# Zero products between the steps at the beginning of the experts: 24, 6, 15 and 14 in place of 14, 4 and 8

## The reference, cut to what matters

```python
def moe_swiglu(x, w_router, w_in, w_out):
    xf = x.reshape(B * S, D)
    logits = (xf @ w_router).astype(jnp.float32)
    top_v, top_i = lax.top_k(logits, TOP_K)          # TOP_K = 2
    w = jax.nn.softmax(top_v, axis=-1)
    gate = jnp.sum(jax.nn.one_hot(top_i, N_EXPERTS) * w[..., None], axis=1)
    out = jnp.zeros((B * S, D), jnp.float32)
    for e in range(N_EXPERTS):
        out = out + gate[:, e:e + 1] * swiglu(xf, w_in[e], w_out[e])
    return out.reshape(B, S, D)
```

## Time and profile before

| | us |
|---|---|
| median of 3 runs | 2832.63 (2832.41 to 2834.3) |
| profiled execution, its own time | 2832.4 |
| its span in the trace | 2830.6 |
| mean granted TensorE clock | 0.968 of full |
| PE busy | 2676.8 (95%) |
| DVE busy | 2113.2 (75%) |
| ACT busy | 1615.6 (57%) |

### The profile page before, as it was taken

The page is one execution under the profiler, slowest core; times in us unless marked ns, Lnnn a source line. Parts: engine busy times, 40 slices in busy tenths (PEclk is TensorE's granted clock), DMA queues, the critical chain, the costliest instruction groups (busy, mean ns, idle before and its releaser), DMA issues.

```text
span 2830.6 us, 39691 instructions
## 1 busy us (share of the span) xinstructions
PE 2676.8 (95%) x12900; PEld 2161.0 (76%) x12900; DVE 2113.2 (75%) x2501; ACT 1615.6 (57%) x2109; POOL 21.5 (1%) x39
## 2 busy tenths in 40 slices
PE   7899999988999999999999888999999999999997
PEld 5677778776777787877997666788878878888875
DVE  6765677676666756866546856699989888999998
ACT  3545544455554444444444543577778777777776
POOL 0000000000000000000000000000000000000000
PEclk9999999999999999999999978899999999999999
DMA  8655468665454655644554411899989999999995
GB/s 315 208 163 167 157 225 263 224 194 176 171 164 142 231 180 177 201 145 157 190 181 156 144 38 45 289 360 335 362 310 366 331 349 336 343 355 331 364 353 214
DMA packets 193794, 666.09 MB, mean 235 GB/s; under 512 B 23056, under 2 KB 34960, under 8 KB 193024
## 3 DMA queue, kind: packets, MB, share of 16 engines
q1 hardware_dynamic: 189760, 647.66, 65.6%
q0 software_dynamic: 3904, 16.76, 1.8%
HBM read 663.29 MB, written 1.05 MB: 235 GB/s over the span
## 4 chain that ended last, share of the span: by engine, by line
PE 81%; DVE 9%; ACT 4%; DVEq 2%; issue 2%; DMA 1%; SPq 0%; ACTq 0%
PE ps L467 45%; PE ps L473 22%; DVE wlo L1971 3%; PE ps L487 2%; PE ps L566 2%; ACT whi L1383 1%; PE ps L492 1%; DVE mod_sum L1995 1%; PE ps L1263 1%; DMA ada_raw<-in_w_ada 1%; PE ps L665 1%; PE ps L777 1%; DMA proj<-in_w_ada 1%; PE ps L707 1%; DVEq L2422 0%
## 5 line engine op out<-in xcount | busy, mean ns | idle before, releaser
L1971 DVE TENSOR_TENSOR wlo<-raw,whi 128x1024 fp32r<-128x1024 f32 x709 | 862.2, 1224 | 445.4 <-ACT whi L1383 433.3
L1383 ACT ACTIVATE whi<-raw 128x1024 fp32r<-128x1024 f32 x709 | 746.1, 1059 | 664.4 <-PE ps L473 588.4
L467 PE MATMUL ps<-whi,xh 128*128 128x512 f32 (+3 forms) x1248 | 454.4, 374 | 4.0 <-issue 4.0
L467 PE MATMUL ps<-whi,xl 128*128 128x512 f32 (+3 forms) x1248 | 443.1, 365 | 0.0
L467 PE MATMUL ps<-whi,gathered_hi 128*128 128x512 f32 x896 | 362.6, 405 | 5.3 <-ACT whi L1383 2.8
L467 PE MATMUL ps<-whi,gathered_lo 128*128 128x512 f32 x896 | 356.0, 397 | 0.0
L473 PE MATMUL ps<-wlo,xh 128*128 128x512 f32 (+3 forms) x1248 | 293.9, 362 | 0.0
L473 PE MATMUL ps<-wlo,gathered_hi 128*128 128x512 f32 x896 | 283.3, 397 | 0.1
L467 PEld LDWEIGHTS ps<-whi,xh 128*128 128x128 f32 x1248 | 239.2, 192 | 43.8 <-issue 6.1
L467 PEld LDWEIGHTS ps<-whi,xl 128*128 128x128 f32 x1248 | 239.8, 192 | 36.3 <-issue 1.7
L473 PEld LDWEIGHTS ps<-wlo,xh 128*128 128x128 f32 x1248 | 216.4, 191 | 38.8
(11 more groups left out here) (420 smaller groups left out, 3586.9 us busy)
## 6 DMA issues: line engine op xcount, KB each, us to landing
raw<-in_moe_w_in SPq DMA_DIRECT2D x227, 512.0 KB, 5.1
spare<-in_moe_w_in SPq DMA_DIRECT2D x165, 512.0 KB, 5.4
mod_b<-in_moe_w_out SPq DMA_DIRECT2D x165, 512.0 KB, 5.3
raw<-in_w_ff SPq DMA_DIRECT2D x128, 512.0 KB, 4.3
raw<-in_w_in SPq DMA_DIRECT2D x96, 512.0 KB, 3.5
work<-in_moe_w_in SPq DMA_DIRECT2D x56, 512.0 KB, 5.2
work<-in_moe_w_out SPq DMA_DIRECT2D x56, 512.0 KB, 4.8
ada_raw<-in_w_ada SPq DMA_DIRECT2D x48, 512.0 KB, 4.5
```

What stands on the lines that cost most here:

```text
L467: e.matmul(ps[0:lhs[2], banks[t], at:at + width], part[:, k0 + j, t * P:t * P + lhs[2]], whi[:, slot, w], start=first and j == 0 and part ...
L1383: e.activation(whi[:, slot, :], src, ACT.Copy).then_inc(split_hi, 1)
L1971: e.tensor_tensor(wlo[:, slot, :], src, whi[:, slot, :].bitcast(F32), ALU.subtract).then_inc(split_lo, 1)
```

## The change

The tuple of counts gets a fourth member and larger numbers. The first group, between the turns of the two tiles, has 24 zero products where it had 14. A new group of 6 stands behind the turns of the second tile, ahead of the wait for `xl`. The group ahead of the wait for the selection has 15 where it had 4, and the group ahead of the wait for the first one-hot rows has 14 where it had 8. All in all there are 59 zero products from `idle` instead of 26.

```diff
-IDLE = (14, 4, 8)
+IDLE = (24, 6, 15, 14)
@@ experts (PE)
                 tile_turns(src, 0)(e)
                 idle(IDLE[0])
                 tile_turns(src, 1)(e)
+                idle(IDLE[1])
                 turned(e)
                 clear(e)
@@
                     job(e, lambda e, bank: e.transpose(ps[:, bank, 0:N_EXP], logitT[:, t * P:(t + 1) * P],
                                                        ident[0:N_EXP, 0:N_EXP]))
-                idle(IDLE[1])
+                idle(IDLE[2])
                 source(e)
@@
                     job(e, fill)
-                idle(IDLE[2])
+                idle(IDLE[3])
                 source(e)
                 n_rounds = 1 if e is SILENT else e.value_load(rounds[0:1, 0:1], min_val=1, max_val=2)
```

## The result

| | before | changed |
|---|---|---|
| median of 20 runs each | 2832.46 us | 2836.45 us |
| lowest and highest | 2827.18 to 2837.24 | 2830.64 to 2843.79 |
| span of the profiled execution | 2830.6 | 2834.0 |
| mean granted clock | 0.968 | 0.968 |

The changed kernel takes 1.0017 times as long (95% interval 1.0011 to 1.0024): 4.0 us more by the medians, where 4.6 us was forecast (2837.0 us against the first profiled execution's 2832.4).

A forecast was written before the change was run, and what follows sets the result against it. PE was taken to set the pace, its beginning being one chain. Terms 0 + 0.85 + 1.2 + 2.5 gave 4.6 us on 2832.4, so 2837.0 us; own range 2834.6 to 2838.4, 8-in-10 range 2829.5 to 2840.0.

The forecast's parts named there:

- The bound: PE sets the pace from 1815 to 2800 us, so a microsecond won or lost before 1815 arrives at the end whole.
- What decides, the clock: All turns on whether zero products keep or restore full clock; the forecast took that they don't, chance 0.43.
- The reservation made there: The half-clock stretch from 1767.0 to 1774.4 includes 14 small products of 8 columns, so it is no clean test.
- The other side's argument: The clock stayed at 1.00 through the first 14 zeros, though 1.4 us of real work stood just before.
- Group 1: 24 zeros for 14 before the second tile's turns: cost nothing, 0.17 us left; 1.0 us if the clock fell early.
- Group 2: Six new zeros ahead of the router, at half clock: 0.85 us late; a slower router, 0.8 us more, only a bound.
- Group 3: 15 zeros for 4 before the selection, the clock falling about halfway: 1.2 us late, bounds 0.2 to 1.8.
- Group 4: 14 zeros for 8 before the gather, already on the path: six more at half clock cost 2.5 us.
- Behind the gather: The gather and the first units run at half clock as before; nothing else is added.
- Rival 1: Zeros count and the clock stays full: 9.1 us faster, or 6.4 with one fall, 2823 to 2826; chance 0.16.
- Rival 2: Group 3 at half clock from its start: 3.3 us late instead of 1.2, total 6.7, 2839.1 us; chance 0.20.
- Rival 3: Zeros hold full clock for a time but not in group 4: 1.4 us gained, 2831.0 us; chance 0.18.

The follow-up runs named there:

- last_only: One-row zero products in group 4 alone, counts 0, 0, 0, 14, against the kernel before's 14, 0, 4, 8; ratio to before 0.9999.
- ones_1_row: Changed kernel's counts (24, 6, 15, 14), each filling product one row of ones in place of zeros; ratio 1.0019 to the kernel before.
- zeros_128_rows: Changed kernel's counts (24, 6, 15, 14), each zero product with 128 rows in place of one; ratio 0.9968 to the kernel before, median 2820.68 us.
- rows128_last_only: Zero products of 128 rows in group 4 alone, counts 0, 0, 0, 14, against the kernel before; ratio 0.9979.

## Why the prediction was right

**The bound.** PE's beginning was one chain, and the four groups cost at the gather nearly what was summed. That a loss "arrives at the end whole" was not borne out by this pair of traces: of 4.87 us at the gather 2.67 were left at the scatter and 1.70 at the end. PE busy for 980.91 of 985 us does not exclude this. The loss that came back lay in stretches where PE was busy at half clock and in a wait for ACT.

**What decides, the clock.** The forecast stood on the reading that one-row zeros don't do for the clock what real products do, from PE busy at half clock for 7.4 us. It held, and the runs show what the forecast left open: with 128 rows in place of one the same counts had a granted clock of 1.00 in all stretches (ratio 0.9968 against 1.0017). Why rows matter they don't show. The reservation made there (8-column products in the stretch) can now be dropped for the zeros: group 4 in last_only is 5.9 us of one-row products and nothing else, at a granted clock of 0.50 throughout, and in the same group with 128 rows it went from 0.50 to 1.00. The other side's argument, full clock through the first 14 zeros, had more real work ahead of it than the 1.4 us named there: PE was busy with real products for all of the 22.04 us from 1728.00 to 1750.04, at 1.00.

**Group 1: 0 forecast, 0 measured** in the profiled execution (6.34 us from turns to turns in both). The reserve was too small: in ones_1_row the clock fell within the group and it cost 2.9 us, not 1.0. Executions of the changed kernel that took up to 2843.79 us may come from this; that is not shown, as no trace of one was taken.

**Group 2: 0.85 forecast, 1.18 measured** (router 10.91 against 9.73). The six zeros began 1.90 us after the second turns, where I had counted 1.7. The router itself then ran at half clock for all of its 24 products, 4.87 us from first to last where it was 4.27. That and its last product's longer duration make the logits' turns another 0.75 us later, 1.93 in all; I had kept this as a bound of 0.8 and taken 0.

**Group 3: 1.2 forecast, 0.38 measured** (places 2.31 us later, less 1.93). I took a fall halfway. The clock, which had risen late, at the end of the router, stayed at 1.00 for the whole group (1767.4 to 1770.7). The two errors belong together: the clock rose later than before (at 1767.3, before at 1762.3) and fell later too.

**Group 4: 2.5 forecast, 2.56 measured** (gather 4.87 us later, less 2.31). **Sum: 4.55 forecast, 4.87 measured** at the gather. It comes so close by luck: groups 2 and 3 were off by +1.08 and -0.82 us, in opposite directions.

**Behind the gather** I expected the same half clock as before. Up to the scatter the delay shrank to 2.67 us. Two things made it shrink. The first units ran at half clock for a shorter time (from 1790.1 to 1794.7 in the changed kernel, from 1783.4 to 1789.6 before). And the kernel before had one more stretch at half clock, behind a wait of 1.83 us for DVE that ended at 1799.5. The changed kernel had the same wait (1.84 us, to 1805.5), and its clock stayed at 1.00 (before, then changed):

```profile
1799.90:1803.20 3.30, 3.30 (x9) 2.59 (x8) 1.70 (x2) 1.34 (x2) 0.00 (x0) 0.50 0.97 365
```

```profile
1794.80:1810.00 15.20, 13.36 (x58) 10.42 (x56) 12.44 (x13) 11.06 (x13) 0.00 (x0) 1.00 0.79 264
```

Behind 1815 another 1 us came back, as shown above. In which waits the clock falls differs from trace to trace. Over 20 runs of each kernel the medians differ by 4.0 us. That is near the forecast 4.6, but this pair of traces shows 1.7 from the first turns to the end, so the full path of the 4.0 us is not shown; how near the number came is in part luck. The direction, and the loss at the gather by the added zeros at half clock, are shown.

**The rivals.** Rival 1's sum is that of another kernel: its 9.1 us is what 128 rows give (ratio 0.9968, so 0.0032 of 2832 us). Its limits by DVE were about right as well: DVE keeps the router to 0.64 us earlier (I said 0.5), the places to 1.48 (1.2), the gather to 2.8 (3.1). Rival 2 did not happen in the profiled execution, since group 3 ran at full clock. Rival 3 is what 64 rows did: full clock up to the places, then a fall in group 4.

For rival 1 spoke only that no gap is left. Filled waits alone did not keep the clock: in group 1 PE was busy to nearly the same extent with 128 rows and with one (5.25 of 5.30 us and 5.30 of 5.30), and behind it the granted clock stayed at 1.00 with 128 rows and was 0.50 with one, as with 32.

## What to carry to other kernels

With all four groups filled by products of 128 rows the granted clock stayed at 1.00 here (zeros_128_rows), and 14 of them in group 4 alone brought it from 0.50 to 1.00 (rows128_last_only); with 1 or 32 rows it was 0.50 behind group 1 and through group 4. Rows cost it no time: 24 fillers took 5.3 us with 1, 32, 64 or 128 rows at full clock. Rows are not enough by themselves: the gather's products have 128 rows and 128 moving columns, PE was busy with them for 7.10 of 7.10 us in the kernel before, and the granted clock stayed at 0.50. Judge a filler by the granted clock behind it, not by PE's busy share, and use the wait's full-clock length for the count only once the clock is known to hold; at half clock the same count is twice as long (14 of them took 6.15 us instead of 3.18) and stands in front of real work. Where it doesn't hold, taking the fillers out is the better kernel (0.9991 against 1.0017 here), and with 128 rows it is the fastest version of this study (0.9968).

## What the runs showed of the hardware

- In the changed kernel the granted clock fell behind a stretch with PE busy for 5.30 of 5.30 us, and it stayed at 0.50 through 6.90 us of unbroken one-row products.
- Ones or zeros made no difference: the ratios are 1.0019 and 1.0017 with one row, and 0.9968 for both with 128 rows (127 of them ones, or all zeros).
- From 0.50, 14 fillers of 128 rows raised the clock within the group (0.50 in its first 2.6 us, 1.00 after); 14 of one row did not in 5.9 us.
- 64 rows held the clock through three groups and lost it in the fourth (one trace, ratio 0.9992); 32 rows lost it as 1 row does (one trace, ratio 1.0012).
- In the changed kernel's trace a loss of 4.87 us at the gather was 1.70 us at the end, though PE was busy for 99.6% of the time from 1815 to 2800 us.
